# Recurrence gates as 64x64 tiles on the four quarters of the array

## The reference

```python
def rg_lru(xc, h0, start, w_rg, b_rg, w_ig, b_ig, lru_lambda):
    xblk = xc.reshape(B, S, N_LRU_BLOCKS, LRU_BLOCK)          # 16 blocks of 64 channels
    r = sigmoid(einsum('bshi,hij->bshj', xblk, w_rg).reshape(B, S, D_RNN) + b_rg)
    i = sigmoid(einsum('bshi,hij->bshj', xblk, w_ig).reshape(B, S, D_RNN) + b_ig)
    log_a = -LRU_C * r * softplus(-lru_lambda)
    a = exp(log_a)
    mult = sqrt(maximum(1.0 - exp(2.0 * log_a), 0.0))
    bterm = mult * i * xc          # then a scan h = a * h_before + bterm over the tokens
```

## Time and profile before

| | |
|---|---|
| median of three runs | 1226.68 us |
| the profiled execution: its own time | 1226.38 us |
| its span in the trace | 1224.4 us |
| busy: TensorE / VectorE / ScalarE / GpSimd | 1182.0 / 392.3 / 225.8 / 83.8 us |
| mean share of the DMA engines' time, 306 to 460 us | all of it, at 427 GB/s |
| TensorE's granted clock, mean over the span | 0.99 |

### The profile page before, as it was taken

The page is one execution under the profiler, slowest core; times in us unless marked ns, Lnnn a source line. Parts: engine busy times, 40 slices in busy tenths (PEclk is TensorE's granted clock), DMA queues, the critical chain, the costliest instruction groups (busy, mean ns, idle before and its releaser), DMA issues.

```text
span 1224.4 us, 16211 instructions
## 1 busy us (share of the span) xinstructions
PE 1182.0 (97%) x6479; PEld 669.2 (55%) x6479; DVE 392.3 (32%) x664; ACT 225.8 (18%) x388; POOL 83.8 (7%) x244
## 2 busy tenths in 40 slices
PE   8999999999999999899999989999999998999996
PEld 7999999985535354334434343544435343553532
DVE  4648586753353413021211111221211121221122
ACT  5533773133101010001101010101101010110111
POOL 4100000010201001101100010101001010110000
PEclk9999999999999999899999999999999999999998
DMA  7543226598999999999999999999999999999993
GB/s 230 169 159 110 96 104 249 184 345 346 428 427 427 427 427 425 422 428 427 424 429 425 427 423 421 421 425 427 427 427 426 426 425 429 426 425 428 426 422 160
DMA packets 54592, 443.71 MB, mean 362 GB/s; under 512 B 5324, under 2 KB 5420, under 8 KB 23536
## 3 DMA queue, kind: packets, MB, share of 16 engines
q1 hardware_dynamic: 53152, 439.91, 86.9%
q0 software_dynamic: 1216, 2.68, 1.0%
q10 hardware_dynamic: 144, 0.04, 0.0%
HBM read 440.63 MB, written 1.98 MB: 361 GB/s over the span
## 4 chain that ended last, share of the span: by engine, by line
PE 81%; DMA 14%; issue 2%; SPq 1%; DVE 0%; POOLq 0%; POOL 0%; ACTq 0%; ACT 0%
PE ps L1697 29%; PE ps L1759 17%; DMA wexp<-in_w_gate_up_dram 11%; PE ps L1595 7%; PE ps L1334 7%; PE ps L1335 7%; PE ps L1336 7%; DMA fnb<-in_final_norm_g_dram 2%; PE ps L1611 2%; PE ps L1612 1%; PE ps L1645 1%; SPq L485 1%; PE ps L1440 1%; PE ps L1603 1%; PE ps L1709 1%
## 5 line engine op out<-in xcount | busy, mean ns | idle before, releaser
L1697 PE MATMUL ps<-wexp,xt 128*64 128x512 f32 (+1 forms) x2048 | 463.7, 604 | 16.4 <-DMA wexp<-in_w_gate_up_dram 10.8
L1697 PEld LDWEIGHTS ps<-wexp,xt 128*64 128x64 f32 (+1 forms) x2048 | 144.0, 132 | 263.3 <-issue 261.6
L1759 PE MATMUL ps<-wexp,act_t 128*64 128x512 f32 (+1 forms) x1104 | 227.2, 593 | 6.1 <-issue 4.2
L1759 PEld LDWEIGHTS ps<-wexp,act_t 128*64 128x64 f32 (+1 forms) x1104 | 81.0, 131 | 137.4 <-issue 137.3
L1249 DVE TENSOR_TENSOR y<-y,ps 128x1024 f32<-128x1024 f32 x51 | 60.8, 1219 | 213.8 <-PE ps L1612 204.9
L818 ACT ACTIVATE g<-g 128x512 f32<-128x512 f32 x33 | 20.8, 630 | 545.1 <-DVE g L1263 545.1
L1334 PE MATMUL ps<-act_h,split 128*128 128x384 f32 x352 | 117.9, 335 | 0.0
L1336 PE MATMUL ps<-act_h,split 128*128 128x384 f32 x352 | 117.6, 334 | 0.0
L1335 PE MATMUL ps<-act_l,split 128*128 128x384 f32 x352 | 117.6, 334 | 0.0
L1595 PEld LDWEIGHTS ps<-pick,xn 128*128 128x128 f32 x768 | 91.1, 196 | 15.3 <-issue 15.3
L1595 PE MATMUL ps<-pick,xn 128*128 128x128 f32 x768 | 94.1, 283 | 2.2 <-POOL pick L581 2.2
(11 more groups left out here) (325 smaller groups left out, 972.0 us busy)
## 6 DMA issues: line engine op xcount, KB each, us to landing
wexp<-in_w_gate_up_dram SPq DMA_DIRECT2D x92, 2048.0 KB, 24.3
wexp<-in_w_down_dram SPq DMA_DIRECT2D x48, 2048.0 KB, 25.8
wexp<-in_w_gate_up_dram SPq DMA_DIRECT2D x38, 1024.0 KB, 25.9
wexp<-in_w_down_dram SPq DMA_DIRECT2D x20, 1024.0 KB, 12.8
raw<-in_w_in_dram SPq DMA_DIRECT2D x19, 1024.0 KB, 5.1
wexp_low<-in_w_gate_up_dram SPq DMA_DIRECT2D x17, 1024.0 KB, 23.9
wexp_high<-in_w_gate_up_dram SPq DMA_DIRECT2D x16, 1024.0 KB, 23.4
wexp_low<-in_w_down_dram SPq DMA_DIRECT2D x5, 1024.0 KB, 21.1
```

The costliest lines, as they stand in the source:

```text
L1697: i_ = pe.matmul(ps[s0:s0 + w, b, :], xt[:, k, s0:s0 + w], weights(k, x)[:, at_:at_ + UC], start=k == 0, stop=k == CB - 1)
L1759: i_ = pe.matmul(ps[s0:s0 + w, 6 + c, :], act_, weights(CB + m, x)[:, D * kk + UC * c:D * kk + UC * c + UC], start=k == 0, stop=k == CB - 1)
```

## The change

Each 64x64 block is now a matmul of its own, on a quarter of the array. For 128 channels there are four: the r gate's two blocks on the quarters of the diagonal, into the upper and lower half of the partitions of a bank of 4 to 7, and the i gate's two blocks on the other two quarters, so that in the bank of 0 to 3 the two halves of the partitions come out exchanged. ScalarE puts them back: the i gate's sigmoid of 128 channels is two instructions of 64 partitions each. `lruw` holds only the blocks, and isn't set to zero any more. All counts are finer: TensorE increments `gates_mm` for each 128 channels (both gates together) and waits for the evacuation of each bank of the chunk before, ScalarE increments `gates_read` for each bank, and what overwrites a bank waits for that bank.

```diff
-            pool.memset(lruw[:], 0.0).then_inc(zeroed, 1)
...
             def sigmoids(hf):
                 for k, (dst, r) in enumerate(((lru_r, BRG_R), (lru_i, BIG_R))):
-                    act.wait_ge(gates_mm, 2 * hf + k + 1)
                     for b in range(4):
+                        act.wait_ge(gates_mm, 4 * hf + b + 1)
                         bank = 4 * (1 - k) + b
...
-                        i_ = act.activation(dst[:, b], ps[:, bank, 0:T], ACT.Sigmoid, bias=cols[:, col:col + 1])
-                    i_.then_inc(gates_read, 1)
+                        if k == 0:
+                            i_ = act.activation(dst[:, b], ps[:, bank, 0:T], ACT.Sigmoid, bias=cols[:, col:col + 1])
+                        else:
+                            for to, at_ in ((slice(0, 64), slice(64, P)), (slice(64, P), slice(0, 64))):
+                                i_ = act.activation(dst[to, b], ps[at_, bank, 0:T], ACT.Sigmoid, bias=cols[to, col:col + 1])
+                        i_.then_inc(gates_read, 1)
...
             def lru_gates(hf):
 
-                for k in range(2):
-                    if hf == 0:
-                        pe.wait_ge(z_evac, 4 * (6 + k))
-                    elif k == 0:
-                        pe.wait_ge(vmix_read, 1)
-                    else:
-                        pe.wait_ge(z_evac, 4 * 8)
-                    for b in range(4):
-                        i_ = pe.matmul(ps[:, 4 * (1 - k) + b, 0:T], lruw[:, k, 4 * hf + b, :], xc[:, 4 * hf + b, :], start=True, stop=True)
+                if hf == 0:
+                    pe.wait_ge(z_evac, 4 * 6)
+                else:
+                    pe.wait_ge(vmix_read, 1)
+                for b in range(4):
+                    pe.wait_ge(z_evac, 4 * (6 + hf) + b + 1)
+                    for k in range(2):
+                        for q in range(2):
+                            rows_, to = slice(64 * q, 64 * q + 64), 64 * (q if k == 0 else 1 - q)
+                            i_ = pe.matmul(ps[to:to + 64, 4 * (1 - k) + b, 0:T], lruw[rows_, k, 4 * hf + b, :],
+                                           xc[rows_, 4 * hf + b, :], start=True, stop=True)
                     i_.then_inc(gates_mm, 1)
...
-            pe.wait_ge(gates_read, 1)
             for g in range(MG):
+                pe.wait_ge(gates_read, g + 1)
...
-            z_chunk(6, 0, 12 + Z_U, lambda b: pe.wait_ge(gates_read, 2))
+            z_chunk(6, 0, 12 + Z_U, lambda b: pe.wait_ge(gates_read, 4 + b + 1))
             lru_gates(1)
-            z_chunk(7, 1, 14 + Z_U, lambda b: pe.wait_ge(gates_read, 3))
-            z_chunk(8, 2, 16 + Z_U, lambda b: pe.wait_ge(gates_read, 4))
+            z_chunk(7, 1, 14 + Z_U, lambda b: pe.wait_ge(gates_read, 8 + b + 1))
+            z_chunk(8, 2, 16 + Z_U, lambda b: pe.wait_ge(gates_read, 12 + b + 1))
```

More of the change, by code:

```diff
@@ L198, in hawk_gmlp_moe_streaming_step @@
         y = at("y", 189440, [P, TT, D])
-        lruw = at("lruw", 201728, [P, 2, CB, P])
+        lruw = at("lruw", 201728, [P, 2, CB, P // 2])
         fnb = at("fnb", RING_AT[(PLACES[LAST] + 7) % RINGS], [P, D])
@@ L377, in _ @@
                 if n == PB_U:
-                    sp.wait_ge(gates_mm, 4)
+                    sp.wait_ge(gates_mm, 2 * 4)
                     load_expert(0)
@@ L515, in _ @@
                                pattern=[[-1, P]], channel_multiplier=1).then_inc(const_ready, 1)
-            pool.memset(lruw[:], 0.0).then_inc(zeroed, 1)
             pool.memset(ws_raw[:, 1], 0.0).then_inc(zeroed, 1)
             pool.memset(xpad[:, :, 0:CW - 1], 0.0).then_inc(const_ready, 1)
-            pool.wait_ge(zeroed, 2)
+            pool.wait_ge(zeroed, 1)
             pool.wait_ge(mix_landed[0], 16)
@@ L553, in _ @@
                 for q in range(2):
-                    pool.dma_start(lruw[64 * q:64 * q + 64, k, :, 64 * q:64 * q + 64],
+                    pool.dma_start(lruw[64 * q:64 * q + 64, k, :, :],
                                    w.rearrange("o (c q) i j -> q i (o c) j", q=2)[q]).then_inc(lruw_loaded, 16)
             pool.dma_start(brb[:], b_router.broadcast_to([P, NE])).then_inc(late_loaded, 16)
-            pool.wait_ge(gates_mm, 4)
+            pool.wait_ge(gates_mm, 2 * 4)
             pool.dma_start(n2p.rearrange("p (m k) -> p m k", k=2), norm2_g.rearrange("o (m p k) -> p (o m) k", k=2, p=P)).then_inc(bias_loaded, 16)
@@ L714, in sigmoids @@
                             act.wait_ge(st_packed, 1)
-                        i_ = act.activation(dst[:, b], ps[:, bank, 0:T], ACT.Sigmoid, bias=cols[:, col:col + 1])
-                    i_.then_inc(gates_read, 1)
+                        if k == 0:
[4 more added lines that the diff above has]
+                        i_.then_inc(gates_read, 1)
             def decays(hf):
                 act.wait_ge(lam_ready, 1)
-                act.wait_ge(gates_read, 2 * hf + 1)
+                act.wait_ge(gates_read, 8 * hf + 4)
                 for b in range(4):
@@ L947, in lru @@
                 cs = slice(4 * hf, 4 * hf + 4)
-                dve.wait_ge(gates_read, 2 * hf + 2)
+                dve.wait_ge(gates_read, 8 * hf + 8)
                 link(dve.tensor_tensor(lru_i[:], lru_i[:], xc[:, cs], ALU.mult))
```

## The result

| | before | after |
|---|---|---|
| median | 1226.03 us (22 runs) | 1227.87 us (22 runs) |
| ratio, 95% interval | | 1.0016 (1.0009 to 1.0022) |
| the profiled execution: its own time / span | 1226.38 / 1224.4 us | 1226.58 / 1224.5 us |

The change costs about 0.16%, 2.0 us, by the interval between 1.1 and 2.7 us. The forecast was 1226.3 us, 0.4 us faster than the kernel before; the time lies in the range, but the small movement has the other sign and is clear of its interval.

What follows compares the result with a forecast made beforehand. TensorE was taken to bound the kernel; of about 5.2 us saved, 2.1 went to waiting for low(19), 1.8 to pauses, some 0.9 to r waits and hand-offs, leaving -0.4: 1226.3 us, range 1225.2 to 1228.9.

Steps and rivals of the forecast that it cites:

- Where the time is decided: At the mixer's end TensorE sets unit 19's start, one to one with the end; low(19) allows under a microsecond gain.
- I take the full price: ScalarE's i gate: 64 partitions cost what 128 do, 0.47 us apart; twelve sigmoids take 5.75 us per half.
- The rival that had this: The i gate's halves don't overlap on ScalarE: 0.88 us more in each half, +1.3 us, 1228.0 us; chance 0.08.
- TensorE's sum: Four quarters work at once: 0.645 us per 128 channels, 2.58 us per half instead of 5.16.
- The pauses around the second gates: TensorE waits about 1.0 us for chunk 6's evacuation before the second gates and 0.8 us before chunk 7.
- Two quarters at a time: Rival: pairs writing one bank run one after the other, 1.29 us per 128 channels; +2.2 us, 1228.9 us; chance 0.12.
- all of them in series: Rival: all four quarter matmuls run one after another, 10.3 us per half; +12.5 us, 1239 us; chance 0.04.
- The clock: Rival: the clock falls to 0.50 after the wait before unit 19, losing 1.7 us; +1.3 us, 1228.0 us; chance 0.22.
- A fall after the pauses around the gates: The same clock loss after pauses around the gates would be absorbed by the wait for low(19).
- the finer waits: Counts and waits per 128 channels, costed at nothing since they satisfy waits earlier.
- the zeroing: GpSimd's zeroing of `lruw`, costed at nothing since GpSimd's next wait is for a DMA.
- The weight transfers: Four weight transfers, costed at nothing since bytes and size of piece stay the same.

Runs made afterwards that it cites:

- whole banks: The changed kernel with each i gate bank read by one 128-partition sigmoid, i gate applied to wrong halves: 1223.03 us, ratio 0.9972 to the kernel before.
- low(19) early: The changed kernel with high(19) ahead of the second square root and low(19) made during VectorE's wait for it: 1224.19 us, ratio 0.9984 to the kernel before.
- both early: The low(19) early kernel plus high(17) ahead of its square root and a looser wait for the second r sigmoids: 1222.14 us, ratio 0.9971 to the kernel before.

## Why the prediction was right or wrong

**Where the time is decided** was right. TensorE bound the kernel before; with faster gates low(19) is late for unit 19, and a pause stands there (2.82 us, 1.9 forecast). What it gains or loses there goes to the end one to one, as far as the intervals of about 1 us either way can tell: unit 20 moved by +1.43, -3.42, -1.71 and -3.47 us in the traces of after, whole banks, low(19) early and both early, and the time by +2.0, -3.4, -2.0 and -3.6 (ratios of 1.0016, 0.9972, 0.9984 and 0.9971). In the other five kernels whose trace shows no fallen clock between the gates and unit 20, the two agree within 0.7 us. From unit 20 to the end of the span it is 1029.7 us before, 1029.5 after, and between 1028.8 and 1031.1 in all fourteen traces.

**The step that failed** is ScalarE's, "I take the full price": the i gate's half was given the spacing of the whole sigmoids, 0.47 us, by VectorE's rows. A half does cost what a whole one does (a record of 0.58 us), but the spacing is another quantity, and no row of before spoke of it for alternating partitions. It is 0.60 us, which makes 0.88 us more in each half. With the longer step from r to i, ScalarE's twelve take 139.70 - 132.94 = 6.76 us in the first half and 6.81 in the second instead of 5.75; less the 0.08 us by which they start earlier than forecast, that is the 1.94 us by which low(19) missed its forecast (2.09 us later than before, 0.15 forecast). The rival that had this, with +1.3 us, had a chance of 0.08 and should have had as much as the forecast: nothing in the trace told the two apart. Its mechanism is the one that came: unit 20 moved by 1.43 us.

**TensorE's sum** was right: four quarters at a time (2.58 us and 0.2 of running out forecast, 2.81 measured). The pauses around the second gates were forecast with 1.0 and 0.8 us; 1.87 and 0.60 stood there, because the evacuation of chunk 6 is behind the longer sigmoids of the first half: it begins 23.82 us after the first gates, and 22.90 was forecast.

**Two quarters at a time** did not happen, and all of them in series did not either. The rule of the Trainium skill, TensorEngine Tiling (Array Packing), "Gotcha 1: PSUM Pressure", that different row tiles cannot access a bank simultaneously, did not show here: the pairs on one bank come from different rows, and four quarters took 0.65 us together. Here each row tile writes its own half of the partitions.

**The clock** was a rival at 0.22, with +1.3 us in all. It did fall, after 1.88 and 2.82 us without work, in some executions and not in others. That adds to the chain's 1.43 us: over the three traces of the change unit 20 is (1.43 + 3.02 + 1.90) / 3 = 2.1 us later than before, and the median ratio says 2.0. That the clock makes up the 0.5 us beyond 1.43 is an estimate from three traces, and the interval of the time, from 1.1 us on, has room for none; that the chain alone costs about 1.4 is shown. A fall after the pauses around the gates was to be absorbed by the wait for low(19): in the one trace that has it, 0.47 of the 1.69 us got through.

**Costed at nothing** and shown so within the intervals: the finer waits and the zeroing. The weight transfers were not tried by themselves.

## What to carry to other kernels

An edit that makes TensorE's part shorter but adds instructions to another engine has to be summed along that engine's chain, to the point where TensorE next waits for it, and the sum must use the spacing of those very instructions. When a fix like this loses, look first for work of the engines behind that can be put into their own waits: here three conversions moved ahead (high(17), high(19) and low(19)) and one looser wait turned a loss of 2.0 us into a gain of 3.6.

## What the runs showed of the hardware

- On ScalarE, sigmoids of 64 partitions from PSUM took 0.58 us each, as those of 128. They started 0.60 us apart when consecutive ones worked on different halves of the partitions, and about 0.47 us when on the same half. Reading partitions 64 to 127 and writing 0 to 63 left the eight at 4.75 us, but behind a sigmoid of 128 partitions the first half began 0.16 us later when it read from partition 64 than when it read from partition 0.
- Four float32 matmuls of 64x64 on 384 columns, on the four quarters, two of them into each of two banks, took 0.65 us together (sixteen in 2.81 us, with some 0.2 of running out); two at a time, on the diagonal alone, 1.3 us for four (sixteen in 5.38 us).
- The granted clock fell to 0.50 after pauses of 1.88, 2.04, 2.64 and 2.82 us, in one execution each, and stayed at 1.00 after 2.82 us in two others of much the same program, and after 1.87 us in three.
